# One matmul of 512 columns for the high and low halves of the activation, in the second feed-forward's first layer

## What is computed

```python
h = rmsnorm(x, g_pre_ffn[l]) * (1.0 + sc2) + sh2
u = jax.nn.relu(h @ w_ff1[l])          # 1024 x 4096
y = (u * u) @ w_ff2[l]                 # 4096 x 1024
x = x + ga2 * rmsnorm(y, g_post_ffn[l])
```

## Time and profile before

| | us |
|---|---|
| median of 3 runs | 778.67 (778.62 to 779.0) |
| the profiled execution | 778.56 |
| its span in the profile | 776.8 |
| PE busy | 744.2 (96%) |
| DVE busy | 544.6 (70%) |
| ACT busy | 380.5 (49%) |

### The profile page before, as it was taken

One profiled execution on the slowest core, in us unless ns is written; L12 is line 12 of the kernel. 1 busy time (PEld: TensorE's weight loads), 2 busy tenths in 40 slices (PEclk: granted clock), 3 DMA queues, 4 the chain that ended last, 5 costly groups with the idle time before them and its releaser, 6 DMA issues.

```text
span 776.8 us, 13201 instructions
## 1 busy us (share of the span) xinstructions
PE 744.2 (96%) x5350; PEld 686.4 (88%) x5350; DVE 544.6 (70%) x901; ACT 380.5 (49%) x524; POOL 51.8 (7%) x72
## 2 busy tenths in 40 slices
PE   5999998989999999998999999999989999999996
PEld 5999986779999999987999999999878999999995
DVE  6797778656677776866669977884767785555554
ACT  6433867655343334446444446656435444444442
POOL 2940000000000000000432000000000000000000
PEclk9999899999999999999999999999998999999999
DMA  8636311439788788661354556445522756445611
GB/s 326 218 121 233 143 55 56 146 125 368 302 312 314 294 319 327 224 239 54 139 195 129 197 222 219 173 163 170 210 108 109 271 217 217 170 167 204 216 55 54
DMA packets 27022, 151.10 MB, mean 195 GB/s; under 512 B 3128, under 2 KB 7836, under 8 KB 9564
## 3 DMA queue, kind: packets, MB, share of 16 engines
q1 hardware_dynamic: 22620, 124.81, 44.5%
q10 hardware_dynamic: 3456, 25.17, 8.1%
q0 software_dynamic: 896, 0.43, 0.3%
HBM read 148.92 MB, written 1.05 MB: 193 GB/s over the span
## 4 chain that ended last, share of the span: by engine, by line
PE 82%; DVE 11%; ACT 3%; issue 2%; DMA 1%; SPq 0%; DVEq 0%; ACTq 0%
PE ps L452 25%; PE ps L453 25%; PE ps L454 25%; DVE ada L1567 3%; DVE w_lo L1469 2%; PE ps L582 1%; PE ps L558 1%; ACT w_hi L1073 1%; PE ps L947 1%; PE ps L516 1%; DMA resid<-x 1%; DVE rows_ga L1613 1%; PE ps L670 0%; PE ps L894 0%; PE ps L525 0%
## 5 line engine op out<-in xcount | busy, mean ns | idle before, releaser
L1469 DVE TENSOR_TENSOR w_lo<-raw,w_hi 128x2048 fp32r<-128x2048 f32 (+1 forms) x109 | 246.7, 2269 | 114.0 <-ACT w_hi L1073 113.8
L452 PE MATMUL ps<-h_hi,w_hi 128*128 128x256 f32 x1064 | 304.8, 286 | 4.1 <-DVE h_lo L1512 1.6
L453 PE MATMUL ps<-h_lo,w_hi 128*128 128x256 f32 x1064 | 301.8, 284 | 0.0
L454 PE MATMUL ps<-h_hi,w_lo 128*128 128x256 f32 x1064 | 301.7, 284 | 0.0
L1073 ACT CAST w_hi<-raw 128x2048 fp32r<-128x2048 f32 (+1 forms) x109 | 203.9, 1887 | 48.7 <-PE ps L454 43.9
L452 PEld LDWEIGHTS ps<-h_hi,w_hi 128*128 128x128 f32 x1064 | 203.5, 191 | 8.5 <-issue 4.4
L453 PEld LDWEIGHTS ps<-h_lo,w_hi 128*128 128x128 f32 x1064 | 203.6, 191 | 1.9 <-issue 0.7
L454 PEld LDWEIGHTS ps<-h_hi,w_lo 128*128 128x128 f32 x1064 | 203.4, 191 | 0.3
L452 PE MATMUL ps<-w_hi,mix_hi 128*128 128x512 f32 x248 | 97.7, 394 | 1.0 <-DVE small L1613 0.8
L453 PE MATMUL ps<-w_lo,mix_hi 128*128 128x512 f32 x248 | 96.8, 391 | 0.0
L454 PE MATMUL ps<-w_hi,mix_lo 128*128 128x512 f32 x248 | 96.5, 389 | 0.0
(11 more groups left out here) (275 smaller groups left out, 875.9 us busy)
## 6 DMA issues: line engine op xcount, KB each, us to landing
raw<-wts SPq DMA_DIRECT2D x113, 1024.0 KB, 4.8
ada<-w_ada ACTq DMA_DIRECT2D x24, 1024.0 KB, 5.2
resid<-x SPq DMA_DIRECT2D x2, 512.0 KB, 4.3
raw<-wts SPq DMA_DIRECT2D x2, 512.0 KB, 6.3
rows_ga<-rows_wide SPq DMA_DIRECT2D x1, 1024.0 KB, 6.8
out<-resid SPq DMA_DIRECT2D x4, 256.0 KB, 2.1
shared<-shared SPq DMA_DIRECT2D x2, 320.0 KB, 7.4
raw<-w_idx SPq DMA_DIRECT2D x1, 544.0 KB, 3.7
```

Source lines behind the costliest of these rows:

```text
L452: nc.tensor.matmul(o, lh, rh, start=start, stop=False)
L453: nc.tensor.matmul(o, lh, rl, start=False, stop=False)
L454: return nc.tensor.matmul(o, ll, rh, start=False, stop=stop)
L1469: V.tensor_tensor(w_lo[:, s % RING, 0:w], raw[:, n_of[name] % RAW, 0:w], w_hi[:, s % RING, 0:w].bitcast(F32), ALU.subtract).then_inc(w_rea ...
```

## The change

`h_hi` and `h_lo` become two halves of one tensor, `h_all`, so that the high and the low part of a slice lie side by side. For the tiles fa0 to fa14 the two matmuls that share the weights `w_hi` (on `h_hi` and on `h_lo`) become one of 512 columns, which writes a whole bank: the product with the high part in its first half, that with the low part in its second. The third matmul (`w_lo` on `h_hi`) stays at 256 columns and adds into the first half. The two halves c go to two banks, 4 and 5 (6 and 7 in step 1). ACT then copies the second halves of both banks into `ff_act` (`keep_low`), DVE adds the first halves to it (`pair_sum`), and the relu reads this sum from SBUF. PE may write the banks again once the sum is done (`sum2_done`). Step 15 keeps the three matmuls and goes to bank 6. `sum_ada(20)` to `(23)` move from steps 0 to 3 into steps 1 to 4, and the two `load_ada` from after steps 0 and 1 to after steps 1 and 2.

```diff
-        h_hi = sb("h_hi", [P, DC, T], F32R)
-        h_lo = sb("h_lo", [P, DC, T], F32R)
+        h_all = sb("h_all", [P, DC, 2, T], F32R)
+        h_hi, h_lo = h_all[:, :, 0, :], h_all[:, :, 1, :]
...
+        pair_bank = lambda st: 6 if st == 1 else 4
...
+            def feature_pair(slot, bank, ready=None):
...
+                        nc.tensor.matmul(ps[:, bank + c, :], wh[:, k, cs], h_all[:, k, :, :].rearrange("p a t -> p (a t)"), start=(k == 0), stop=False)
+                        i = nc.tensor.matmul(ps[:, bank + c, 0:T], wl[:, k, cs], h_hi[:, k, :], start=False, stop=(k == DC - 1))
...
-                if st >= 3:
-                    pe.wait_ge(relu2_done, i * 3 + (st - 2))
-                feature_tile(s0 % RING, 4 + st % 3, h_hi, h_lo, 4 * DC if st == 0 else None).then_inc(pe_tile, 1)
+                if st >= 2:
+                    pe.wait_ge(sum2_done, pair_free or i * 3 + st)
+                feature_pair(s0 % RING, pair_bank(st), 4 * DC if st == 0 else None).then_inc(pe_tile, 1)
...
-            ff2_step(2)
+            ff2_step(2, pair_free=1)
...
-            pe.wait_ge(relu2_done, 13)
-            feature_tile(s % RING, 4 + 15 % 3, h_hi, h_lo).then_inc(pe_tile, 1)
+            feature_tile(s % RING, 6, h_hi, h_lo).then_inc(pe_tile, 1)
...
+                return nc.scalar.copy(o.rearrange("p (c t) -> p c t", c=2), ps[:, bank:bank + 2, T:2 * T])
...
-                nc.scalar.activation(ff_act[st % 3], ps[:, 4 + st % 3, :], ACT.Relu).then_inc(relu2_done, 1)
+                if st < FF2_STEPS - 1:
+                    keep_low(ff_act[st % 3], pair_bank(st)).then_inc(low2_done, 1)
+                    act.wait_ge(sum2_done, i * 3 + (st + 1))
+                src = ff_act[st % 3] if st < FF2_STEPS - 1 else ps[:, 6, :]
+                nc.scalar.activation(ff_act[st % 3], src, ACT.Relu).then_inc(relu2_done, 1)
...
-                if st < 2:
-                    load_ada(22 + st)
+                if 1 <= st < 3:
+                    load_ada(21 + st)
...
+                o = o.rearrange("p (c t) -> p c t", c=2)
+                return V.tensor_tensor(o, o, ps[:, bank:bank + 2, 0:T], ALU.add)
...
+                if st < FF2_STEPS - 1:
+                    dve.wait_ge(low2_done, i * 3 + (st + 1))
+                    pair_sum(ff_act[st % 3], pair_bank(st)).then_inc(sum2_done, 1)
...
-                if st < 4:
-                    sum_ada(20 + st)
+                if st >= 1:
+                    sum_ada(19 + st)
```

More of the change, by code:

```diff
@@ L274, in build @@
         silu_done, hid_done, hidhi_done, hidlo_done = (sem(n) for n in ("silu_done", "hid_done", "hid_hi_done", "hid_lo_done"))
+        low2_done, sum2_done = sem("low2_done"), sem("sum2_done")
         relu2_done, hid2_done, hid2hi_done, hid2lo_done = (sem(n) for n in ("relu2_done", "hid2_done", "hid2_hi_done", "hid2_lo_done"))
@@ L471, in feature_tile @@
                                 k == 0, k == DC - 1)
+                return i
+            def feature_pair(slot, bank, ready=None):
+                wh, wl = w3(slot, DC)
+                for c in range(2):
+                    cs = slice(c * P, (c + 1) * P)
+                    for k in range(DC):
+                        if ready is not None and c == 0:
+                            pe.wait_ge(h_ready, ready + k + 1)
+                        nc.tensor.matmul(ps[:, bank + c, :], wh[:, k, cs], h_all[:, k, :, :].rearrange("p a t -> p (a t)"), start=(k == 0), stop=False)
+                        i = nc.tensor.matmul(ps[:, bank + c, 0:T], wl[:, k, cs], h_hi[:, k, :], start=False, stop=(k == DC - 1))
                 return i
@@ L1000, in _, with ff2_step @@
             norm_turn(3)
-            def ff2_step(st, i=0, first=False):
+            def ff2_step(st, i=0, first=False, pair_free=None):
                 s0 = s_idx[f"fa{st}"]
                 pe.wait_ge(w_ready, i * 6 + (s0 + 1))
-                if st >= 3:
-                    pe.wait_ge(relu2_done, i * 3 + (st - 2))
-                feature_tile(s0 % RING, 4 + st % 3, h_hi, h_lo, 4 * DC if st == 0 else None).then_inc(pe_tile, 1)
+                if st >= 2:
+                    pe.wait_ge(sum2_done, pair_free or i * 3 + st)
+                feature_pair(s0 % RING, pair_bank(st), 4 * DC if st == 0 else None).then_inc(pe_tile, 1)
                 if st >= 1:
@@ L1063, in load_ada, with keep_low @@
                 act.dma_start(ada[:, t % 2, :], src).then_inc(s_ada[t % 2], 16)
+            def keep_low(o, bank):
+                return nc.scalar.copy(o.rearrange("p (c t) -> p c t", c=2), ps[:, bank:bank + 2, T:2 * T])
             def split(s, name, i=0):
@@ L1463, in link, with pair_sum @@
                 dve.wait_ge(dstep, steps[0])
+            def pair_sum(o, bank):
+                o = o.rearrange("p (c t) -> p c t", c=2)
+                return V.tensor_tensor(o, o, ps[:, bank:bank + 2, 0:T], ALU.add)
             def split(s, name, i=0):
```

## The result

| | before | after |
|---|---|---|
| median of 22 runs each, us | 778.19 (776.6 to 779.95) | 779.66 (778.0 to 781.36) |
| ratio, 95% interval | | 1.0021 (1.0013 to 1.0029) |
| profiled execution, us | 778.56 | 778.92 |
| its span, us | 776.8 | 777.1 |

The changed kernel is slower by 0.21%, 1.6 us, on the very edge of what can be told from no change. The same kernel was run again later, twelve times beside twenty runs of the kernel before, and gave 1.0013 (1.0000 to 1.0026). The forecast was 0.8 us slower.

The account below looks back on a forecast made before the run. PE was taken to bound the kernel, with DVE slower for four steps after the change. Waits of 3.70 us less 2.93 saved gave 0.8 slower: 778.56 + 0.78 + 0.11 = 779.4 us, range 777.3 to 781.9.

Parts of the forecast that it names:

- the outcome called likeliest: Whole kernel: no change that a measurement can tell, 777.1 to 780.2 us, given a chance of 0.62.
- what PE gains: Tiles fa0 to fa14: 0.0125 us per merged pair, 0.20 a full tile, 2.93 us in total.
- sum's start to square's start: DVE and ACT, each step: sum, relu and square in line add 1.35 us to every round of DVE.
- gain behind fb5: PE, the eight merged tiles fa7 to fa14: they give 1.60 us back after fb5's late start.
- DVE's times: DVE, steps 0 to 5: sums, squares and splits timed link by link, sum 0 at 595.63 to fb5's split done at 658.73.
- DVE sets fb5: Up to tile fb5 DVE sets the time; savings before it are lost in waits, and fb5 starts 2.38 us later.
- The waits: PE waits for DVE before fa4, fb3, fb4, fa6 and fb5, 3.70 us in sum, the longest 1.70 before fa6.
- The rule of the Trainium skill: Merged pairs on PE: columns' time plus about 2.5 ns would save 2.5 ns a pair, 0.6 us in all; the forecast rejected it.
- Slow handovers: Rival, sum 0 to sum 5: 24 DVE-ACT handovers at 0.12 instead of 0.03 us, 2.2 more, 781.6; chance 0.14.
- The clock falls in the wait: Rival, PE's 1.70 us wait before fa6: a slow-clock stretch adds 1.5 us, 781.0; chance 0.05.
- A looser chain: Rival, DVE's early rounds: some 0.75 us shorter each, PE never waits and keeps 2.93, 775.7; chance 0.12.
- A matmul less saves almost nothing: Rival, merged tiles: fa takes about its old time, only 0.3 us returns behind fb5, 2.1 more, 780.8; chance 0.03.

Follow-up runs that it names:

- experiment 1: Changed kernel with the merged matmul taken apart into two of 256 columns, copies and sums kept: 780.66 us, ratio 1.0032 to the kernel before.
- 5: Changed kernel with the modulation's bias and gains moved from after step 4 to after the loop: 777.48 us, ratio 0.9995 to the kernel before.
- 6: Changed kernel with ACT's two modulation loads issued behind the copy of steps 2 and 3: 777.47 us, ratio 0.9998 to the kernel before.
- 9: Changed kernel with ACT's relu folded into DVE's square in steps 0 to 14: 776.40 us, ratio 0.9977 to the kernel before.
- Experiment 2: Changed kernel with each half tile's eight 512-column matmuls first, then its eight of 256, fa0 included: 780.70 us, ratio 1.0035 to the kernel before.
- the second trace of the grouped kernel: Changed kernel with matmuls grouped by width in all merged tiles, fa0 too, executed once more, unchanged: 779.86 us in one run.

## Why the prediction was right, step by step

The time (779.4 forecast, 779.66 measured) and the outcome called likeliest hold. That the two times lie so close is in part luck. The forecast was 0.8 us slower, and the change measured 1.5 by the medians and 1.6 by the ratio, about twice that. The forecast stood on a median of 3 runs (778.67) that lies 0.48 above that of the 22 (778.19), which made up for most of the 0.7 by which the difference fell short. The mechanism held, and one term of its sum, what PE gains, was too large. The steps, from fa0:

| step | forecast | after |
|---|---|---|
| sums 0 to 5 start | 8.41, 15.15, 27.52, 39.89, 51.13, 64.42 | 8.40, 15.17, 27.56, 40.00, 51.27, 64.63 |
| sum's start to square's start | 1.35 | 1.38 |
| waits: fa4, fb3, fb4, fa6, fb5 | 0.37, 0.57, 0.22, 1.70, 0.84 | 0.14, 0.45, 0.05, 1.72, 0.54 |
| fb5 starts | 71.73 | 71.55 |
| a merged tile, undisturbed | 5.56 | 5.64 |
| gain of all tiles | 2.93 | about 1.7 |
| fb5 later than in before | 2.38 | 2.20 |
| gain behind fb5 | 1.60 | 0.78 |

- **DVE's times** were right within 0.21 us over 56 us, and with them the place and the releaser of every wait. They had been worked out from distances between rows of before, link by link; where a row was missing (the add, the copy, the relu from SBUF) the nearest form served: add 0.68 for 0.68, copy 0.59 for 0.59, relu 0.63 for 0.60. The 0.03 more of the relu in each round is most of the 0.2.
- **That DVE sets fb5** and the merge gains nothing before it: shown by experiment 1 (71.55 with and without the merge), and by 5, 6 and 9, which each shorten that chain and bring fb5 forward by 2.1 to 3.2.
- **The waits** sum to 3.13, with 0.11 and 0.12 for the late second matmuls of fb3 and fb5, where 3.70 was forecast. (Here the time by which a tile and the start behind it exceed an undisturbed one counts as a wait.) They are smaller mainly because PE was later by itself: its tiles were 0.08 longer than forecast. Also, fa6 started 0.06 behind the end of the sum (651.60 to 651.66), where 0.15 was forecast, and its second matmul came 0.10 late, where 0.07 was. What PE loses in a wait and what it loses in its own pace are the same time here.
- **What PE gains** is the term that was mis-sized. The step was "per pair 0.240 - 0.2275 = 0.0125 us; 16 pairs a tile make 0.20". The pitch of 256 was read where all neighbours have that width, and that of 512 as the mean of a tile fb, of which only the first five starts are longer. By turns, a 256 starts 0.236 behind a 512 and a 512 0.117 behind a 256, 0.3525 together instead of 0.3475. So a pair gains 0.0075, a tile 0.12 (0.114 over the eight steps). Experiment 2 shows that it is the order: with the widths grouped the tile takes the forecast 5.56. Behind fb5 the eight tiles give 0.91 instead of 1.60. The tile fb5 itself is 0.13 longer by its late second matmul, so 0.78 is left: 0.82 short. fb5 itself came 0.18 earlier than forecast. From fa0 to fa15 that makes 0.78 + 0.82 - 0.18 = 1.42 later, which is what the trace has.
- **The rule of the Trainium skill against the rows.** Joining two 256s saved 7.5 ns a pair by turns and 12.5 ns grouped, by the pitches above. The formula for the isolated gap in the Trainium skill (TensorE: Matmul & The Clock Gate, section Back-to-back issue gap), which adds about 2.5 ns to the columns' time, would make it 2.5 ns. The measurement decides: the rule is too small here in either order.

**The rivals.** *Slow handovers* did not come: in the written-out steps relu and square still begin 0.03 after what they wait for. *The clock falls in the wait* did not come either. The stretches on both sides of fa6's start (columns as in the earlier trace rows):

```profile
650.00:652.00 2.00, 0.55 (x3) 0.30 (x3) 1.60 (x7) 0.36 (x1) 0.00 (x0) 1.00 0.62 258
652.00:658.00 6.00, 5.74 (x33) 4.76 (x32) 3.90 (x4) 4.83 (x5) 0.00 (x0) 1.00 0.00 0
```

PE was busy for 0.55 of 2 us, and the clock stayed at 1.00 there and behind. *A looser chain* was not there; experiments 5, 6 and 9 had to make it. *A matmul less saves almost nothing* was refuted as it stood, but the saving was only 0.12 of the 0.20. No rival asked what a changed neighbour does to the pitch of a matmul.

## What to carry to other kernels

Less work on one engine is worth nothing as long as another engine sets its pace. Before merging work on the busiest engine, lay the helper's round (here DVE's) next to it link by link, with side work and loads in it. Then give the added steps to the part of the loop where the round has room, or remove a link in exchange (here the relu, folded into the square). Read an instruction's pitch where its neighbours are those that it will have, and put matmuls of equal width together, but not in a tile whose operands still arrive one at a time. A load whose issue waits for another engine belongs behind the work that somebody waits for, not ahead of it.

## What was not expected of the hardware

- **Alternating widths cost 0.005 us a pair of matmuls.** 512 and 256 columns by turns took 0.3525 a pair, eight and eight 0.3475. Over a tile of 16 pairs that is 0.08. It was seen in five kernels by turns (5.64) and in five grouped ones (5.56), without exception. The longer pitch is that of 512s close behind a 256 (1.16 for the first five of a tile fb, 1.13 for the next five). Why is open; the traces show only the starts.
- **The granted clock fell in the middle of fa0, behind a stretch in which PE lacked work.** In the second trace of the grouped kernel it was 1.00 with PE busy for 1.03 of 2 us in fa0, and 0.52 and 0.63 in the four microseconds behind, in which there was work. By turns PE was busy for 1.33 of the same 2 us in after, and the clock stayed at 1.00. Before fa6 an idle time of 1.45 us behind full work left it at 1.00 too. What tells these apart was not tried.
- **A scalar_tensor_tensor on 128x512 floats took the 0.69 of a plain product**, so the maximum in it cost nothing here.
